# A two-layer decoder trunk: gains and shifts of the residual on GpSimd reordered around the next weight splits, and part of a normalisation moved to ScalarE

## The chip, the cores and the metric

The kernel runs on one core of a Trainium2 chip. The metric is device time in microseconds (us) of one execution, lower is better. The kernel before takes 2448.8 us, the median of three runs (2448.49 to 2449.93). The profile comes from one further execution of 2449.08 us, whose span from the first to the last instruction is 2447.4 us. The engines are named by their short names in the profile: PE is TensorE, PEld its weight load, DVE is VectorE, ACT is ScalarE, POOL is GpSimd, SP is SyncE.

## The reference

Two layers (DEPTH = 2) work on 1024 positions of width 1024. Layer 0 mixes by dilated attention, layer 1 by a spatial gating unit (SGU); both have a cross attention into 256 memory rows, and both end in a SwiGLU feed-forward network (FFN) of width 2816. Every sum is followed by a layer norm.

```python
def layer_norm(x, g, b):
    y = (x - mean(x)) * rsqrt(var(x) + 1e-5)
    return y * g + b

def causal_chunk_sgu(u, v, ln_g, ln_b, w_s, b_s):      # layer 1, width 768
    v = layer_norm(v, ln_g, ln_b)
    mixed = einsum('gts,bnsgc->bntgc', tril(w_s), v in chunks of 128, 12 groups of 64) + b_s
    return u * mixed

for i in range(2):
    ...                                                # mix = attention or SGU of x @ w_in
    y = concatenate([mix, memory_attention]) @ w_out[i]
    x = layer_norm(DN_ALPHA * x + y, ln_mix_g[i], ln_mix_b[i])
    f = (silu(x @ w_gate[i]) * (x @ w_up[i])) @ w_down[i]
    x = layer_norm(DN_ALPHA * x + f, ln_ffn_g[i], ln_ffn_b[i])
```

DN_ALPHA is the square root of 2. What the change touches is the end of the first layer norm of each layer (times g, plus b, then times DN_ALPHA and plus f), and the layer norm of v in the SGU.

## The kernel before, in words

**Numbers.** Every fp32 product is made of three matmuls in a rounded type: both operands are split into a high and a low part, and high·high, low·high and high·low are added in PSUM (`three`, lines 262 to 266). Weights come from HBM in units of 128 x 1024 into a ring of two raw buffers (`load`), and GpSimd splits each unit into `Wh` and `Wl` by two instructions (`split`, lines 253 and 256). A load waits until the unit two before it has been split. Activations are split by ScalarE (high) and VectorE (low).

**Residual.** `XR` holds x as 8 tiles of 128 x 1024. After the output projection it is normalised in place (`out_norm_dve`, `out_norm_act`): ScalarE writes (x - mean) * rstd (line 1018). TensorE then transposes it (line 902), ScalarE and VectorE apply gain and shift by column on the transposed side and split it into `XTh` and `XTl` (`row_act`, `row_dve`). The row-wise gain and shift of `XR` itself, which only the residual sum needs, are done by GpSimd (`norm_pool`, lines 1056 and 1060, with the rows in `gb`) once all 16 pieces of `XTl` are written.

**FFN.** It runs in 11 chunks of 256 hidden columns. A chunk c takes six weight units: gate and up for two column blocks (j = 0 to 3) and two units of w_down (j = 4, 5). TensorE makes four pairs of gate and up (i = 0 to 3, `ffn_pe`), ScalarE the silu (1166) and the high part (1172), VectorE the product `hid` (1179) and the low part (1186). Then TensorE makes 16 products with w_down, and VectorE adds each to `XR` (`acc_dve`): in chunk 0 with the old `XR` times ALPHA (line 870), later by a plain addition (872). Before a pair i, TensorE waits for the `gated` of pair i - 2. The w_gate and w_up slots of a chunk are free for the next chunk's split once the `up` product of its second half is done (`used`).

**SGU.** `wide_pe` makes 24 products of 256 columns for v and then 24 for u. ScalarE applies gelu to v into the 8 tiles of `V` (1265). VectorE takes statistics and, for tiles 0 to 3 and then 4 to 7, writes (v - mean) * rstd (1332) and the gain (1335); the shift is added by GpSimd for tiles 0 to 3 (1392) and by VectorE for 4 to 7 (1338). Then 12 groups are mixed, between the u products 4 to 8 (`MIX_AT`): per group ScalarE writes `VSh` (1292), VectorE `VSl` (1356, it raises `v_low`), TensorE three matmuls, VectorE adds the bias (`gate`, 1344); u products are taken by gelu into one of two buffers `ub` (1281) and multiplied by VectorE (`gated`, 1351). GpSimd splits the last two units of the u weights only when `v_low` has reached 6.

**Order.** Each engine's program is written out by hand and runs in its order; semaphores join them. Nothing is scheduled by a tool.

Of the kernel before, what the change touches and what calls it, by code (L numbers as in the profile page):

```python
# [20 lines left out]
ALU = mybir.AluOpType  # L21
# [52 lines left out]
def build(nc, a, out):  # L74
# [970 lines left out]
    def norm_pool(pool, g, tiles, done=0, last=False):  # L1045
# [3 lines left out]
        for n, t in enumerate(tiles, done):  # L1049
# [9 lines left out]
            pool.wait_ge(*g("gained", n + 1))  # L1059
            nc.gpsimd.tensor_tensor(XR[:, t, :], XR[:, t, :], shift, ALU.add).then_inc(g("shifted"), 1)  # L1060

    def load_cols(eng, g, gain, shift):
        with nc.allow_non_contiguous_dma(reason="1024 gains and shifts, once"):
            for i, w in enumerate((gain, shift)):
                eng.dma_start(gcol[:, i, :], w.rearrange("(k p) -> p k", p=P)).then_inc(g("col_landed"), 16)
# [10 lines left out]
    class Names:  # L1076
# [5 lines left out]
        def __call__(self, name, value=None):  # L1082
# [3 lines left out]

    NORM = {"row_turned": 2 * KT, "affine": 2 * KT, "odd_high": KT, "even_high": KT, "xt_low": 2 * KT, "stats": NT, "root": NT, "partial": 2 * NT, "inverse": NT,
            "rstd": NT, "normed": NT, "gained": NT, "shifted": NT, "gb_landed": 32,
            "col_landed": 32}
    OUT = {**NORM, "product": 16 * KT // 2, "added": 16 * KT // 2}  # L1090
    FFN = {**NORM, "product": 16 * NCH, "added": 16 * NCH,
           **{x: 4 * NCH for x in ("gate", "up", "silu", "gated", "hid_high", "hid_low")}}
# [164 lines left out]
    def sgu_act(act):  # L1257
        act.wait_ge(*at_("mixed", 40))
        act.dma_start(wsraw[:, :, :], a["sgu_w_s"][0].rearrange("g t s -> t g s")).then_inc(gsg("ws_landed"), 16)
        with nc.allow_non_contiguous_dma(reason="1536 biases, once"):  # L1260
            act.dma_start(bst[:, :], a["sgu_b_s"][0].rearrange("g t -> t g")).then_inc(gsg("bs_landed"), 16)

        for n in range(3 * NT):
            act.wait_ge(*gvp("product", n + 1))
            nc.scalar.activation(channels(n), bank(n % 4, M), ACT.Gelu_apprx_tanh).then_inc(gvp("gelu"), 1)
            if n == 9:
                act.wait_ge(*gsg("ws_turned", 1))
                nc.scalar.activation(WSh[:, :, :], ps[:, 2048:2048 + NG * P].rearrange("p (g t) -> p g t", t=P),
                                     ACT.Copy).then_inc(gsg("ws_high"), 1)
                load_gb(act, gsg, a["sgu_ln_g"][0], a["sgu_ln_b"][0], sgb)  # L1270
            if n >= 2 * NT and n % 4 == 3:
                t0 = n % NT - 3
                act.wait_ge(*gsg("stats", t0 + 4))
                nc.scalar.activation(rstd[:, t0:t0 + 4], mv[:, t0:t0 + 4, 1], ACT.Sqrt,
                                     bias=eps[:, 0:1]).then_inc(gsg("root"), 1)

        def gelu(n):
            act.wait_ge(*gup("product", n + 1))
            if n >= 2:
                act.wait_ge(*gup("gated", n - 1))  # L1280
            nc.scalar.activation(ub[:, n % 2, :], bank(n % 4, M), ACT.Gelu_apprx_tanh).then_inc(gup("gelu"), 1)

        gelu(0)
        gelu(1)
        for n in sorted(MIX_AT):
            for i in MIX_AT[n]:
                if i == 0:
                    act.wait_ge(*gsg("shifted", NT // 2))
                    act.wait_ge(*gsg("shifted_late", NT // 2))
                if i >= 2:  # L1290
                    act.wait_ge(*gsg("spatial", i - 1))
                nc.scalar.activation(VSh[:, i % 2, :, :], V[:, :, i * HD:(i + 1) * HD], ACT.Copy
                                     ).then_inc(gsg("v_high"), 1)
            if n == 5:
                gelu(2)
            if n >= 5:
                gelu(n - 2)
        act.wait_ge(*gsg("spatial", NG))
        load_gb(act, go[1], a["ln_mix_g"][1], a["ln_mix_b"][1], gb)

        def turn(t):
            ts = slice(t * P, (t + 1) * P)
            turn_act(act, gup, t, DIL_W // P, 4)
            nc.scalar.activation(XTh[:, 6:8, ts], MO[:, :, ts], ACT.Copy).then_inc(gup("mo_high"), 1)

        for n in range(7, 3 * NT):
            gelu(n)
            if n >= 2 * NT + 2:
                turn(n - 2 * NT - 2)
        turn(NT - 2)  # L1310
        turn(NT - 1)

    def sgu_dve(dve):
        for n in range(3 * NT):
# [7 lines left out]
            if j == 2:  # L1322
                dve.wait_ge(*gsg("partial", n + 1))
                nc.vector.bn_aggr(mv[:, t, :], st[:, t, :, :].rearrange("p a b -> p (a b)")).then_inc(gsg("stats"), 1)
                if t % 4 == 3:
                    t0 = t - 3
                    dve.wait_ge(*gsg("root", t // 4 + 1))
                    nc.vector.reciprocal(rstd[:, t0:t0 + 4], rstd[:, t0:t0 + 4]).then_inc(gsg("rstd"), 1)
                    dve.wait_ge(*gsg("rstd", t // 4 + 1))
                    dve.wait_ge(*gsg("gb_landed", 32))  # L1330
                    for q in range(t0, t0 + 4):
                        nc.vector.tensor_scalar(V[:, q, :], V[:, q, :], mv[:, q, 0:1], rstd[:, q:q + 1], ALU.subtract,
                                                ALU.mult).then_inc(gsg("normed"), 1)
                        dve.wait_ge(*gsg("normed", q + 1))
                        nc.vector.tensor_tensor(V[:, q, :], V[:, q, :], sgb[:, 0, :], ALU.mult).then_inc(gsg("gained"), 1)
                        if q >= NT // 2:
                            dve.wait_ge(*gsg("gained", q + 1))
                            nc.vector.tensor_tensor(V[:, q, :], V[:, q, :], sgb[:, 1, :],
                                                    ALU.add).then_inc(gsg("shifted_late"), 1)
# [123 lines left out]
    def _(pool):  # L1463
# [23 lines left out]
            split(pool, u, attention_over if U_OUT[0] + 3 <= u < U_OUT[0] + 6 else None)  # L1487

        def ffn_units(L):
            for j in range(4):  # L1490
                split(pool, U_FFN[L] + j)
            for j in range(4, 6):
                split(pool, U_FFN[L] + j)
            pool.wait_ge(*go[L]("xt_low", 2 * KT))
            norm_pool(pool, go[L], range(NT))
            with pool.Fori(1, NCH) as c:
                for j in range(6):
                    split(pool, U_FFN[L] + c * 6 + j, used(U_FFN[L] + j, c - 1), (U_FFN[L] + j) % RS,
                          U_FFN[L] // 2 + c * 3 + j // 2 + 1, slot_of(U_FFN[L] + j))
# [15 lines left out]
        for u in range(U_U, U_U + 4):  # L1515
            split(pool, u)
        sgu_pool(pool)
        pool.wait_ge(*gsg("v_low", 6))
        for u in range(U_U + 4, U_FFN[1]):
            split(pool, u)  # L1520
        ffn_units(1)
# [77 lines left out]
    def _(act):  # L1599
# [11 lines left out]
        for L in range(2):  # L1611
# [11 lines left out]
                sgu_act(act)  # L1623
            load_cols(act, go[L], a["ln_mix_g"][L], a["ln_mix_b"][L])
            out_norm_act(act, go[L])
            ffn_first(lambda j: row_act(act, go[L], j), lambda i: ffn_silu(act, L, 0, i), lambda i: ffn_high(act, L, 0, i))
            load_cols(act, gf[L], a["ln_ffn_g"][L], a["ln_ffn_b"][L]) if L == 0 else None
            act.wait_ge(*go[L]("shifted", NT))
# [43 lines left out]
    def _(dve):  # L1672
# [17 lines left out]
        for L in range(2):  # L1690
# [23 lines left out]
                      lambda i: ffn_low(dve, L, 0, i))  # L1714
            for t in range(NT):

                dve.wait_ge(*go[L]("shifted", t + 1))
                acc_dve(dve, gf[L], 0, t, ALPHA)
            with dve.Fori(1, NCH - 1) as c:
                for i in range(4):  # L1720
                    ffn_gated(dve, L, c, i)
# [59 lines left out]
```

## Time and profile before

| quantity | value |
|---|---|
| median of three runs | 2448.8 us |
| the profiled execution | 2449.08 us |
| its span | 2447.4 us |
| PE busy | 2333.3 us, 95% |
| DVE busy | 998.1 us, 41% |
| ACT busy | 599.7 us, 25% |
| POOL busy | 1012.2 us, 41% |
| mean granted PE clock | 0.983 |

PE is busy nearly all the time, so the other engines matter only where PE stands still for them. A granted clock of 1.00 is full speed, 0.50 half speed.

### The profile page before, as it was taken

Reading aid. Unit: us, or ns where it says so; the run is one execution under the profiler, and the core shown is the slowest. Engines: PE = TensorE matmul, PEld = TensorE weight load, DVE = VectorE, ACT = ScalarE, POOL = GpSimd, SP = SyncE. Lnnn points to the kernel's source line nnn. Section 1 sums busy time; section 2 is a strip of 40 time slices with the busy share of each in tenths; the row PEclk is TensorE's granted clock in tenths of the full one; section 3 lists DMA queues with packets and bytes.
Section 4 is the critical chain, followed back from the end, with each engine's and each line's share of the span. In section 5 each row is a group of like instructions: output and inputs, shape, how many; then the busy total and the mean of one; then the engine's idle time right before and its main releaser. Section 6 shows DMA issues by size and latency. Waiting matters only on the chain.

```text
span 2447.4 us, 29983 instructions
## 1 busy us (share of the span) xinstructions
PE 2333.3 (95%) x11608; PEld 1967.2 (80%) x11608; DVE 998.1 (41%) x1931; ACT 599.7 (25%) x1173; POOL 1012.2 (41%) x462
## 2 busy tenths in 40 slices
PE   7999999899999999999998789889999999999997
PEld 6888888678788888888887689878788888888885
DVE  4555555547322222222227536557422222222226
ACT  4656555504100000000005632213200000000003
POOL 3322112653943444333333663434854433333444
PEclk9999999999999999999999989999999999999998
DMA  4111111131111111111111030211021111111111
GB/s 139 61 46 42 44 44 37 59 112 44 44 60 51 51 51 43 43 49 44 44 52 61 9 95 19 70 35 52 27 77 50 44 44 43 43 51 51 51 35 69
DMA packets 160470, 127.63 MB, mean 52 GB/s; under 512 B 11520, under 2 KB 146304, under 8 KB 160384
## 3 DMA queue, kind: packets, MB, share of 16 engines
q1 hardware_dynamic: 147808, 114.31, 15.1%
q10 hardware_dynamic: 12576, 12.16, 1.5%
q8 instruction: 56, 0.92, 0.2%
q14 instruction: 30, 0.25, 0.0%
HBM read 122.26 MB, written 4.19 MB: 52 GB/s over the span
## 4 chain that ended last, share of the span: by engine, by line
PE 83%; DVE 7%; POOL 4%; issue 3%; ACT 3%; DMA 0%; ACTq 0%; DVEq 0%; POOLq 0%
PE ps L264 25%; PE ps L266 25%; PE ps L265 25%; PE ps L552 2%; POOL XR L1056 2%; POOL XR L1060 2%; PE ps L578 1%; PE ps L579 1%; DVE XTl L941 1%; PE ps L539 1%; PE ps L540 1%; DVE XR L872 1%; DVE st L959 1%; PE ps L830 1%; DVE XTh L938 1%
## 5 line engine op out<-in xcount | busy, mean ns | idle before, releaser
L253 POOL TENSOR_TENSOR Wh<-raw,zcol 128x1024 fp32r<-128x1024 f32 x190 | 363.4, 1913 | 1269.7 <-PE ps L266 1234.1
L264 PE MATMUL ps<-XTh,Wh 128*128 128x512 f32 x1760 | 701.6, 399 | 11.9 <-POOL Wl L256 7.3
L266 PE MATMUL ps<-XTh,Wl 128*128 128x512 f32 x1760 | 689.9, 392 | 0.0
L265 PE MATMUL ps<-XTl,Wh 128*128 128x512 f32 x1760 | 689.9, 392 | 0.0
L256 POOL TENSOR_TENSOR Wl<-raw,Wh 128x1024 fp32r<-128x1024 f32 x190 | 470.4, 2476 | 14.9
L264 PEld LDWEIGHTS ps<-XTh,Wh 128*128 128x128 f32 x1760 | 333.0, 189 | 74.8 <-issue 8.2
L266 PEld LDWEIGHTS ps<-XTh,Wl 128*128 128x128 f32 x1760 | 332.4, 189 | 71.0
L265 PEld LDWEIGHTS ps<-XTl,Wh 128*128 128x128 f32 x1760 | 333.3, 189 | 60.2
L872 DVE TENSOR_TENSOR XR<-XR,ps 128x512 f32<-128x512 f32 x416 | 280.9, 684 | 229.0 <-PE ps L266 228.9
L1179 DVE TENSOR_TENSOR hid<-silu,ps 128x512 f32<-128x512 f32 x88 | 60.5, 687 | 737.8 <-PE ps L266 734.1
L264 PE MATMUL ps<-Wh,hidh 128*128 128x512 f32 x704 | 275.6, 391 | 5.1 <-DVE hidl L1186 2.8
L266 PE MATMUL ps<-Wh,hidl 128*128 128x512 f32 x704 | 275.6, 392 | 0.0
L265 PE MATMUL ps<-Wl,hidh 128*128 128x512 f32 x704 | 275.4, 391 | 0.0
L1166 ACT ACTIVATE silu<-ps 128x512 f32<-128x512 f32 x88 | 52.6, 598 | 777.6 <-PE ps L266 777.6
L264 PE MATMUL ps<-Wh,XTh 128*128 128x256 f32 (+1 forms) x640 | 212.0, 331 | 4.8 <-DVE XTl L843 3.6
L265 PE MATMUL ps<-Wl,XTh 128*128 128x256 f32 (+1 forms) x640 | 210.7, 329 | 0.0
L266 PE MATMUL ps<-Wh,XTl 128*128 128x256 f32 (+1 forms) x640 | 210.5, 329 | 0.0
L1172 ACT ACTIVATE hidh<-hid 128x512 fp32r<-128x512 f32 x88 | 55.6, 632 | 458.0 <-DVE hid L1179 458.0
L264 PEld LDWEIGHTS ps<-Wh,hidh 128*128 128x128 f32 x704 | 133.1, 189 | 33.5 <-issue 5.9
L265 PEld LDWEIGHTS ps<-Wl,hidh 128*128 128x128 f32 x704 | 133.0, 189 | 27.7
L266 PEld LDWEIGHTS ps<-Wh,hidl 128*128 128x128 f32 x704 | 132.8, 189 | 27.7
L264 PEld LDWEIGHTS ps<-Wh,XTh 128*128 128x128 f32 x640 | 123.2, 192 | 16.0 <-DVE XTl L843 3.8
(152 smaller groups left out, 2579.2 us busy)
## 6 DMA issues: line engine op xcount, KB each, us to landing
raw<-in_w_gate SPq DMA_DIRECT2D x44, 512.0 KB, 3.8
raw<-in_w_up SPq DMA_DIRECT2D x44, 512.0 KB, 3.8
raw<-in_w_down SPq DMA_DIRECT2D x44, 512.0 KB, 3.4
raw<-in_a_w_in SPq DMA_DIRECT2D x20, 512.0 KB, 3.8
raw<-in_w_out SPq DMA_DIRECT2D x16, 512.0 KB, 3.4
raw<-in_b_w_in SPq DMA_DIRECT2D x14, 512.0 KB, 3.8
B<-in_c_bias SPq DMA_DIRECT2D x12, 512.0 KB, 3.4
raw<-in_w_mem_kv SPq DMA_DIRECT2D x8, 512.0 KB, 4.6
```

Source lines behind the costliest of these rows:

```text
L253: nc.gpsimd.tensor_tensor(Wh[:, slot, :], raw[:, turn, :], zcol[:, 0:1].to_broadcast([P, UNIT]), ALU.add).then_inc(high_done, 1)
L256: nc.gpsimd.tensor_tensor(Wl[:, slot, :], raw[:, turn, :], Wh[:, slot, :].bitcast(F32), ALU.subtract).then_inc(split_done, 1)
L264: nc.tensor.matmul(dst, wh, xh, start=first, stop=False)
L265: nc.tensor.matmul(dst, wh, xl, start=False, stop=False)
L266: return nc.tensor.matmul(dst, wl, xh, start=False, stop=last)
L552: mm = nc.tensor.transpose(bank(4 + gi % 2, P, x * P), probs_of(g, 2 * s + ab, (lo + k) * P, (lo + k + 1) * P), ident[:, :])
L872: nc.vector.tensor_tensor(x, x, bank(4 + n % 4), ALU.add).then_inc(g("added"), 1)
L1056: nc.gpsimd.tensor_tensor(XR[:, t, :], XR[:, t, :], gain, ALU.mult).then_inc(g("gained"), 1)
L1060: nc.gpsimd.tensor_tensor(XR[:, t, :], XR[:, t, :], shift, ALU.add).then_inc(g("shifted"), 1)
L1166: nc.scalar.activation(silu[:, i % 2, :], bank(2 * (i % 2)), ACT.Silu).then_inc(g("silu"), 1)
L1172: nc.scalar.activation(hidh[:, m, h * 512:(h + 1) * 512], hid[:, i % 2, :], ACT.Copy).then_inc(g("hid_high"), 1)
L1179: nc.vector.tensor_tensor(hid[:, i % 2, :], silu[:, i % 2, :], bank(2 * (i % 2) + 1), ALU.mult).then_inc(g("gated"), 1)
```

## The change

The FFN part, in both layers. GpSimd's order was: splits of chunk 0; gain and shift of tiles 0 to 7 alternately; splits of chunk 1. It is now: splits of chunk 0; eight gains; the splits of the gate and up units of chunk 1; eight shifts; the two w_down splits of chunk 1. Since the sum x = ALPHA * XR + f of chunk 0 now comes before the shift, the shift is added behind it, and its row is multiplied by ALPHA by one new ScalarE instruction. VectorE's first additions wait for the gain alone; both VectorE and ScalarE wait for all eight shifts before their loop over chunks 1 to 9.

The SGU part, in layer 1. For tiles 4 to 7 ScalarE does (v - mean) * rstd in place of VectorE, with a new VectorE instruction that makes -mean * rstd for the four tiles; ScalarE does it ahead of its first two gelus of u. GpSimd splits the last two u units when `v_low` has reached 12, not 6.

```diff
+    def gains_pool(pool, g):
+
+        pool.wait_ge(*g("gb_landed", 32))
+        for t in range(NT):
+            nc.gpsimd.tensor_tensor(XR[:, t, :], XR[:, t, :], gb[:, 0, :], ALU.mult).then_inc(g("gained"), 1)
+
+    def shifts_pool(pool, L):
+
+        pool.wait_ge(*go[L]("gb_scaled", 1))
+        for t in range(NT):
+            pool.wait_ge(*gf[L]("added", 2 * t + 2 + gf[L].credit))
+            nc.gpsimd.tensor_tensor(XR[:, t, :], XR[:, t, :], gb[:, 1, :], ALU.add).then_inc(go[L]("shifted"), 1)
...
+        act.wait_ge(*gsg("nmr", 1))
+        act.wait_ge(*gsg("normed", 4))
+        for q in range(4, NT):
+            nc.scalar.activation(V[:, q, :], V[:, q, :], ACT.Identity, bias=nmr[:, q:q + 1],
+                                 scale=rstd[:, q:q + 1]).then_inc(gsg("normed"), 1)
         gelu(0)
         gelu(1)
...
+                    if t0:
+                        nc.vector.scalar_tensor_tensor(nmr[:, t0:t0 + 4], mv[:, t0:t0 + 4, 0], -1.0, rstd[:, t0:t0 + 4],
+                                                       ALU.mult, ALU.mult).then_inc(gsg("nmr"), 1)
                     for q in range(t0, t0 + 4):
-                        nc.vector.tensor_scalar(V[:, q, :], V[:, q, :], mv[:, q, 0:1], rstd[:, q:q + 1], ALU.subtract,
-                                                ALU.mult).then_inc(gsg("normed"), 1)
+                        if t0 == 0:
+                            nc.vector.tensor_scalar(V[:, q, :], V[:, q, :], mv[:, q, 0:1], rstd[:, q:q + 1],
+                                                    ALU.subtract, ALU.mult).then_inc(gsg("normed"), 1)
...
         def ffn_units(L):
-            for j in range(4):
-                split(pool, U_FFN[L] + j)
-            for j in range(4, 6):
+            for j in range(6):
                 split(pool, U_FFN[L] + j)
             pool.wait_ge(*go[L]("xt_low", 2 * KT))
-            norm_pool(pool, go[L], range(NT))
-            with pool.Fori(1, NCH) as c:
+            gains_pool(pool, go[L])
+            for j in range(4):
+                split(pool, U_FFN[L] + 6 + j, U_FFN[L] + j)
+            shifts_pool(pool, L)
+            for j in range(4, 6):
+                split(pool, U_FFN[L] + 6 + j, U_FFN[L] + j)
+            with pool.Fori(2, NCH) as c:
...
         sgu_pool(pool)
-        pool.wait_ge(*gsg("v_low", 6))
+        pool.wait_ge(*gsg("v_low", NG))
...
             out_norm_act(act, go[L])
+            act.wait_ge(*go[L]("gb_landed", 32))
+            nc.scalar.activation(gb[:, 1, :], gb[:, 1, :], ACT.Copy, scale=ALPHA).then_inc(go[L]("gb_scaled"), 1)
...
             for t in range(NT):
 
-                dve.wait_ge(*go[L]("shifted", t + 1))
+                dve.wait_ge(*go[L]("gained", t + 1))
                 acc_dve(dve, gf[L], 0, t, ALPHA)
+            dve.wait_ge(*go[L]("shifted", NT))
```

The order of GpSimd's instructions where the FFN of a layer begins, in the kernel before. The first row is the low part of the last split of chunk 0, L1056 is a gain, L1060 a shift, and L1496 the start of the loop that splits chunk 1 and later.

```order
L256 TENSOR_TENSOR Wl<-raw,Wh 128x1024 [waits high_done]
L1056 TENSOR_TENSOR XR<-XR,gb 128x1024 [waits out_row_turned,out_gb_landed,out_xt_low]
L1060 TENSOR_TENSOR XR<-XR,gb 128x1024 [waits out_gained]
L1056 TENSOR_TENSOR XR<-XR,gb 128x1024 [waits out_row_turned]
...
L1496 UNCONDITIONAL_BRANCH
L1496 ISA
L251 ISA [waits raw_landed0]
L253 TENSOR_TENSOR Wh<-raw,zcol 128x1024 [waits ffn_up]
```

The same place on GpSimd in the changed kernel, where L1066 is a gain, L1073 a shift and L1521 the start of the loop, which now begins with chunk 2.

```order
L1066 TENSOR_TENSOR XR<-XR,gb 128x1024 [waits out_gb_landed,out_xt_low]
L1066 TENSOR_TENSOR XR<-XR,gb 128x1024 x7
L253 TENSOR_TENSOR Wh<-raw,zcol 128x1024 [waits ffn_up,raw_landed0]
L256 TENSOR_TENSOR Wl<-raw,Wh 128x1024 [waits high_done]
...
L1073 TENSOR_TENSOR XR<-XR,gb 128x1024 [waits ffn_added,out_gb_scaled]
L1073 TENSOR_TENSOR XR<-XR,gb 128x1024 [waits ffn_added] x7
L253 TENSOR_TENSOR Wh<-raw,zcol 128x1024 [waits ffn_product,raw_landed0]
...
L1521 UNCONDITIONAL_BRANCH
```

Four splits of chunk 1 have moved ahead of the eight shifts, and two stand behind them; each shift has gained a wait for VectorE's additions.

ScalarE's instructions in the SGU of the changed kernel, from the square root for tiles 4 to 7 on: L1299 is the new normalisation, L1294 the gelu of u with its table, L1310 the first `VSh`. In the kernel before, the table load followed the square root at once.

```order
L1287 ACT_TABLE_LOAD
L1287 ACTIVATE rstd<-mv,eps 128x4 [waits sgu_stats]
L1299 ACTIVATE V<-V,nmr,rstd 128x768 [waits sgu_normed,sgu_nmr]
L1299 ACTIVATE V<-V,nmr,rstd 128x768 x3
L1294 ACT_TABLE_LOAD
L1294 ACTIVATE ub<-ps 128x256 [waits uproj_product] x2
L1310 ACTIVATE VSh<-V 128x512 [waits sgu_shifted_late,sgu_shifted]
```

VectorE's instructions at the same place: L1357 is the gain of one of the tiles 4 to 7, L1360 its shift, and the new L1350 stands where the first of four normalisations stood.

```order
L1346 RECIPROCAL rstd<-rstd 128x4 [waits sgu_root]
L1350 SCALAR_TENSOR_TENSOR nmr<-mv,rstd 128x4 [waits sgu_gb_landed,sgu_rstd]
L1357 TENSOR_TENSOR V<-V,sgb 128x768 [waits sgu_normed]
L1360 TENSOR_TENSOR V<-V,sgb 128x768 [waits sgu_gained]
L1357 TENSOR_TENSOR V<-V,sgb 128x768 [waits sgu_normed]
```

Each tile now costs VectorE two instructions where it had three, and the two gelus of u stand behind four new ScalarE instructions.

## Rows read from the trace of the kernel before

**Rows 1.** Waits of PE: line and releaser, us in total, times, longest.

```profile
PE ps L264 <- POOL Wl L256: 7.3, 2, 3.7
PE ps L264 <- DVE VSl L1356: 6.9, 5, 2.3
```

**Rows 2.** Timeline of PE, layer 0, chunk 0 to 1: start, duration, [idle before].

```profile
659.37 0.39 PE L266 MATMUL ps<-Wh,hidl 128*128 128x512 f32 x1
663.41 0.79 PE L264 MATMUL ps<-XTh,Wh 128*128 128x512 f32 x1 [3.66 <-POOL Wl L256]
667.03 0.40 PE L264 MATMUL ps<-XTh,Wh 128*128 128x512 f32 x1
```

**Rows 3.** Windows there: length, busy us of PE, PEld, DVE, ACT, POOL, PEclk, DMA.

```profile
660.00:667.00 7.00, 3.59 (x9) 2.86 (x10) 0.48 (x1) 0.00 (x0) 6.84 (x4) 0.76 0.52 150
696.00:740.00 44.00, 44.00 (x195) 36.45 (x195) 14.29 (x20) 2.46 (x4) 26.28 (x12) 1.00 0.20 60
```

**Rows 4.** Timeline of POOL, layer 0: first gain, first two splits of chunk 1.

```profile
614.20 2.36 POOL L1056 TENSOR_TENSOR XR<-XR,gb 128x1024 f32<-128x1024 f32 x1 [17.76 <-DVE XTl L941]
...
654.64 1.89 POOL L253 TENSOR_TENSOR Wh<-raw,zcol 128x1024 fp32r<-128x1024 f32 x1
...
658.97 1.89 POOL L253 TENSOR_TENSOR Wh<-raw,zcol 128x1024 fp32r<-128x1024 f32 x1
```

**Rows 5.** Timeline of DVE, layer 0: last addition of chunk 0, hid of chunk 1.

```profile
659.79 0.69 DVE L870 SCALAR_TENSOR_TENSOR XR<-XR,ps 128x512 f32<-128x512 f32 x1 [0.60 <-PE ps L266]
676.14 0.69 DVE L1179 TENSOR_TENSOR hid<-silu,ps 128x512 f32<-128x512 f32 x1 [15.66 <-PE ps L266]
...
687.02 0.69 DVE L1179 TENSOR_TENSOR hid<-silu,ps 128x512 f32<-128x512 f32 x1 [8.34 <-PE ps L266]
```

**Rows 6.** Timeline of ACT, layer 0: last two normalisations, two groups of row pieces.

```profile
600.74 2.38 ACT L1018 ACTIVATE XR<-XR,nmr,rstd 128x1024 f32<-128x1024 f32 x2
603.94 1.45 ACT L927 ACTIVATE fbuf<-ps,gcol 128x512 f32<-128x512 f32 x2 [0.83 <-PE ps L902]
...
609.11 1.45 ACT L927 ACTIVATE fbuf<-ps,gcol 128x512 f32<-128x512 f32 x2 [1.05 <-PE ps L902]
```

**Rows 7.** Timeline of PE in the SGU: mixes of groups 0, 3 and 11.

```profile
1519.76 0.66 PE L264 MATMUL ps<-VSh,WSh 128*128 128x512 f32 x1 [2.31 <-DVE VSl L1356]
...
1524.00 0.50 PE L264 MATMUL ps<-VSh,WSh 128*128 128x512 f32 x1
...
1548.86 0.50 PE L264 MATMUL ps<-VSh,WSh 128*128 128x512 f32 x1 [1.79 <-DVE VSl L1356]
```

**Rows 8.** Timeline of DVE in the SGU: normalisation, last shift, VSl, gated.

```profile
1507.70 0.68 DVE L1332 TENSOR_SCALAR V<-V,mv,rstd 128x768 f32<-128x768 f32 x1
...
1517.14 0.96 DVE L1338 TENSOR_TENSOR V<-V,sgb 128x768 f32<-128x768 f32 x1
1518.93 1.29 DVE L1356 TENSOR_TENSOR VSl<-V,VSh 128x512 fp32r<-128x512 f32 x2 [0.83 <-ACT VSh L1292]
...
1530.57 3.88 DVE L1356 TENSOR_TENSOR VSl<-V,VSh 128x512 fp32r<-128x512 f32 x2
1534.37 2.61 DVE L1351 TENSOR_TENSOR V<-V,ub 128x256 f32<-128x256 f32 x1
...
1548.73 0.41 DVE L1351 TENSOR_TENSOR V<-V,ub 128x256 f32<-128x256 f32 x1
```

**Rows 9.** Timeline of POOL in the SGU: first and last instruction of four splits.

```profile
1527.03 2.01 POOL L253 TENSOR_TENSOR Wh<-raw,zcol 128x1024 fp32r<-128x1024 f32 x1 [20.25 <-DVE VSl L1356]
...
1545.57 2.69 POOL L256 TENSOR_TENSOR Wl<-raw,Wh 128x1024 fp32r<-128x1024 f32 x1
```

**Rows 10.** Timeline of ACT in the SGU: last gelu of v, table, first VSh.

```profile
1503.10 0.38 ACT L1265 ACTIVATE V<-ps 128x256 f32<-128x256 f32 x1 [2.50 <-PE ps L266]
...
1507.47 1.28 ACT L1281 ACT_TABLE_LOAD   x1
...
1518.19 1.15 ACT L1292 ACTIVATE VSh<-V 128x512 fp32r<-128x512 f32 x2 [8.77 <-DVE V L1338]
```

More of the change, by code:

```diff
@@ L1088, in build @@
             "rstd": NT, "normed": NT, "gained": NT, "shifted": NT, "gb_landed": 32,
-            "col_landed": 32}
+            "col_landed": 32, "gb_scaled": 1}
     OUT = {**NORM, "product": 16 * KT // 2, "added": 16 * KT // 2}
@@ L1330, in sgu_dve @@
                     dve.wait_ge(*gsg("gb_landed", 32))
+                    if t0:
+                        nc.vector.scalar_tensor_tensor(nmr[:, t0:t0 + 4], mv[:, t0:t0 + 4, 0], -1.0, rstd[:, t0:t0 + 4],
+                                                       ALU.mult, ALU.mult).then_inc(gsg("nmr"), 1)
                     for q in range(t0, t0 + 4):
-                        nc.vector.tensor_scalar(V[:, q, :], V[:, q, :], mv[:, q, 0:1], rstd[:, q:q + 1], ALU.subtract,
-                                                ALU.mult).then_inc(gsg("normed"), 1)
+                        if t0 == 0:
+                            nc.vector.tensor_scalar(V[:, q, :], V[:, q, :], mv[:, q, 0:1], rstd[:, q:q + 1],
+                                                    ALU.subtract, ALU.mult).then_inc(gsg("normed"), 1)
                         dve.wait_ge(*gsg("normed", q + 1))
                         nc.vector.tensor_tensor(V[:, q, :], V[:, q, :], sgb[:, 0, :], ALU.mult).then_inc(gsg("gained"), 1)
-                        if q >= NT // 2:
+                        if t0:
                             dve.wait_ge(*gsg("gained", q + 1))
```

## The prediction, made before the changed kernel had run

> **What bounds the kernel now.** I read the page first, for the busy shares: PE is busy 95% of the span, so time can only be won where PE stands still or runs slowly. Next I read PE's waits by releaser. Two of the groups are touched by the change: PE waits twice for GpSimd's weight split, 7.3 us, and five times for the low part VSl in the SGU, 6.9 us [rows 1]. Then I went to these places in the timelines. The rest of PE's waits (attention, the turns between stages) is at lines that the change leaves alone.
>
> The first place is the step from chunk 0 to chunk 1 of each FFN. The last matmul of chunk 0 starts at 659.37, the first of chunk 1 at 663.41, after 3.66 us of idle time released by GpSimd's Wl [rows 2]. After the stop PE also runs slowly: the granted clock is 0.76 over the 7 us that hold the stop, and 1.00 later on [rows 3]. Matmuls of 512 columns follow each other at 0.227 us when PE is warm (44 us of the window 696 to 740 hold 195 records of nearly all such matmuls [rows 3]).
>
> The second place is the mixing of the 12 groups in the SGU. PE waits 2.31 us before group 0 and is held up again until group 11 [rows 7]. VectorE is the engine waited for, and its instructions there are long: two VSl take 1.29 us at 1518.93 but 3.88 us at 1530.57, and one gated takes 0.41 us at 1548.73 but 2.61 us at 1534.37 [rows 8]. What differs is GpSimd, which is idle at 1518.93 and at 1548.73 and splits four units from 1527.03 to 1548.26 [rows 9].
>
> **The change part by part.**
>
> *FFN, the stop of PE.* Before, eight gains and eight shifts occupy GpSimd from 614.20 to 654.64, so 2.53 us each, and a split takes 4.33 us (658.97 - 654.64) [rows 4]. PE needs two splits, ready at 663.3. Now only the eight gains stand ahead: 614.2 + 8 x 2.53 = 634.4. The first two splits end at 634.4 + 2 x 4.33 = 643.1, the third and fourth at 651.8. The slots are free in time: the first two splits need the third pair of chunk 0, the other two the fourth, and all pairs are over before the 16 products, which take 16 x 6 x 0.227 = 21.8 us up to 659.6, so by 637.8. The raw data of the first two units landed long ago; for the third and fourth the same ring at the same pace of 4.33 us applies as after 654.64, where GpSimd shows no wait [rows 4]. PE wants the first two at 659.6, so it has 16 us to spare and goes on without a stop. What is won per layer: 663.41 - 659.37 - 0.23 = 3.81 us of stop, and in the slow stretch 667.03 - 663.41 = 3.62 us for nine matmuls that take 9 x 0.227 = 2.04, so 1.58 us [rows 2]. Together 5.39 us, twice 10.8 us. The step from chunk 1 to 2, at the loop's end, runs with PE busy throughout [rows 3], so I give the loop's start no hidden cost.
>
> *FFN, what is late next.* The eight shifts follow at 651.8. The last needs the addition that ended at 660.5 [rows 5] and is reached at 651.8 + 7 x 2.53 = 669.5, so it waits for nothing; all end at 672.0. Behind that wait stand, on ScalarE, one DMA issue and the silu of chunk 1's pair 0, and on VectorE its hid. The gate product will be ready at 665 and the silu is late by 7 us: hid at about 672.0 + 0.6 + 0.1 = 672.7, over at 673.4. PE asks for it only before pair 2, two pairs after 659.6. A pair takes 10.88 us (687.02 - 676.14 [rows 5]), so at 681.4: 8 us to spare. The two w_down splits end at 672.0 + 8.7 = 680.7, and PE asks for them after four pairs, at 703. Cost 0; with the cover gone each us beyond these margins would be a us of stop. VectorE's own additions are not delayed: the gain of tile t is done by 634.4, and the first of the 16 products is over at 637.8 + 1.36 = 639.2.
>
> *FFN, the new ScalarE instruction.* It has the size of line 1018, 1.19 us each [rows 6]. It starts at 603.12, where ScalarE is idle for 0.83 us, and ends at 604.3, so the first row pieces start 0.37 us late. Before the second group ScalarE waits 1.05 us for PE [rows 6]; the 0.37 goes into that. Cost 0; between 0 and 0.4 us a layer.
>
> *SGU, the normalisation.* Before, VectorE works on tiles 4 to 7 from 1507.70 to 1518.10 [rows 8], and ScalarE starts VSh at 1518.19, after 8.77 us of idle [rows 10]. Now VectorE makes one small instruction (0.2 us, my estimate for four elements a row), to 1507.9. ScalarE's first tile takes 3/4 of 1.19 plus its fixed part, 0.93 us, so the first gain starts at 1508.95. Then VectorE has two instructions of 0.96 us a tile, 8 x 0.96 = 7.7 (0.97 x 8 with the gaps). It ends at 1516.65 and not 1518.10: 1.45 us won. The four ScalarE instructions end at 1511.65, the table load takes 1.28 us [rows 10], and gelu 0 is over at 1513.3. PE needs it before u product 4, which starts four products of 2.88 us after 1502.9 (2.88 is ScalarE's rhythm, 2.50 idle and 0.38 busy [rows 10]), at 1514.4. It is in time by 1.1 us. Cost 0; if these instructions ran at 1.24 us each, still 0.
>
> *SGU, the first four groups.* Mix 0 moves from 1519.76 to 1518.3. PE's idle time before it shrinks from 2.31 to 0.9 us. Mixes 0 to 3 took 4.24 us from start to start (1519.76 to 1524.00 [rows 7]), slower than the 3 x 0.69 they need: partly PE's slow clock after the stop, partly the chain VSh, VSl, mix with two buffers. With the chain at warm speed I count 3.7 us. Won here: 1.45 + 0.55 = 2.0 us. Unknown is whether the clock holds: bounds 1.4 and 2.3.
>
> *SGU, groups 4 to 11.* Now GpSimd waits for the twelfth VSl, so it is idle in this whole stretch. Before, from the end of mix 3 (1524.8) to the end of mix 11 (1549.66, 0.8 after its start in rows 7) are 24.86 us. PE's own work there is four products and eight mixes: 4 x 2.88 + 8 x 0.69 = 17.0. Per product and pair of mixes VectorE has two VSl (1.3), one gated (0.41) and two gates (1.4), 3.1 us against PE's 4.26. So at undisturbed lengths VectorE keeps up, and 7.8 us go. Bounds: nothing from a part of it if the order of the hand-overs matters, so 6 to 7.9.
>
> *SGU, the splits behind it.* PE starts product 5 at 1524.8 - 2.0 = 1522.8; three products and six mixes later, at 1535.6, mix 9 is over, and a gate and two VSl (0.7 and 1.3) bring the twelfth VSl to 1537.6. The four splits took 21.2 us before with collisions (1527.03 to 1548.26 [rows 9]); they now run in 17.4 to 21 us, from 1537.7 to 1556. The first two end at 1546.4; PE needs them for u product 16, eight products after product 8 (which ends at 1538.4, before the last mixes), at 1559.9. In time by 13 us. But these splits now stand beside gated 5 to 10. One of these takes up to 2.61 us [rows 8], less than the 2.88 of a product, and two buffers lie between. I follow the first: gate 11 ends at 1540.7, gated 5 comes through when GpSimd's instruction ends, at 1542.7, gelu 7 at 1543.1, and PE wanted it at 1542.7. Cost 0.4 us, bounds 0 and 2.
>
> By the Trainium skill (SBUF — State Buffer, section SBUF: two separate sides), VectorE with two SBUF inputs and a GpSimd instruction exclude each other: whichever starts first keeps the shared ports for its whole length. The trace agrees: 2.61 us is one GpSimd instruction waited for plus 0.41 of its own. The same page speaks against the change in that it moves the collision rather than removes it; by it alone every gated beside a split would take up to 2.7 us, which is the rival below.
>
> **Sum.** 10.8 + 2.0 + 7.8 - 0.4 = 20.2 us less. From the profiled execution of 2449.08 us that gives 2428.9 us; this execution lies 0.3 us above the median of the runs, so I say 2428.8.
>
> **The rivals.**
>
> *The collision is moved.* Gated and VSl slow down because of GpSimd's splits, and the four splits are still there. If VectorE falls behind in gated 5 to 10 as it did in the mixes, PE loses in this stretch what it lost before, up to 6.3 us. For it: lengths of 2.61 and 3.88 us in rows 8. Against it: there is only one such instruction per 2.88 us of PE's work now, not three. Time: 2428.8 + 6 = 2435.
>
> *Only one of the two parts pays.* The FFN part may be given back if PE meets another wait in chunk 1, such as for pair 2; or the SGU part, if gelu 0 or the table is late. If the FFN part brings half, 2428.8 + 5.4 = 2434; if it brings nothing, 2439.6. Against it are margins of 8 and 16 us.
>
> *The change doesn't do what it says.* The stop at chunk 1 remains, because the splits of chunk 1 wait for raw data or for slots until the shifts are through. The stop would stay 3.66 us, the SGU's 9.4 us would be won: 2439.4. Rows 4 speak against it.
>
> *Slower: the shift gate.* All of chunk 1's silu and hid now stand behind the eighth shift. The hand-over from it to PE's pair 2 takes 1.4 us, so PE stops once the shifts end after 680.0. To eat the 5.4 us of its layer they would have to end at 685.4, and to make the whole kernel slower they must also eat the half of the SGU's gain, 4.7 us, so end after 690.1, 18 us later than the 672.0 worked out. Twenty-four instructions of 1.9 to 2.5 us lie between 614.2 and there, and each would have to take 0.75 us more. The longest collisions in the stretch before are already in its mean of 2.53. If they did end at 693, the time would be 2454.
>
> **How the numbers follow.** The forecast has 0.78, its own range 2426 to 2433: the bounds are 2.3 and 1.4 for the first groups, 7.9 and 6 for the others, 0 and 2 for the moved collision, and 0 to 0.8 for the scaling. The moved collision has 0.09, only one part paying 0.06, the stop that remains 0.03, the shift gate 0.02, and 0.02 is left for causes that I don't see. Differences within 0.2% (4.9 us) of 2448.8 are what a measurement of this kernel can't tell from none. All but the last two cases lie beyond this on the fast side. Faster 0.96, same 0.02, slower 0.02. The range that holds 8 in 10, with the nearer part of the moved collision: 2425 to 2435.
>
> **What would show it.** PE's waits after the change: no line for Wl at the step to chunk 1, and the windows there at clock 1.00. GpSimd: gains from 614.2 to 634.4, four splits to 651.8, shifts to 672.0. VectorE's hid of chunk 1's pair 0 at about 673 and PE without a wait before pair 2. In the SGU: first VSh at 1516.7 less the 5.4 us of layer 0, VSl at 0.65 us each throughout, mix 11 ending near 1539.8 - 5.4, and one or two gated of 2.6 us behind it. It would be wrong if PE shows new waits for gated, gelu or hid, if the four ScalarE tiles take over 1.3 us each, or if the clock falls before mix 0.

## The result and the profile after

The changed kernel takes 2425.11 us, the median of four runs (2424.09 to 2426.58). The kernel before took 2449.36 us in the runs that go with them (2448.49 to 2451.92), so the change takes off 24.2 us. The ratio is 0.990, with a 95% interval of 0.9883 to 0.9917. I had forecast 2428.8 us, which is 20.0 us off the 2448.8 of the table. The direction and both mechanisms held. The gain was 4 us larger than forecast: the measured time lies 0.1 us inside the lower end of my range of 2425, and taken as a ratio of 2448.8 (2424.3) it lies outside. One run of the kernel `fn` below, 3356.55 us at a granted clock of 0.652, is left out of its median.

The page of the changed kernel, busy time by engine, and its chain of waits by engine:

```profile
PE 2323.6 (96%) x11608; PEld 1960.2 (81%) x11608; DVE 996.9 (41%) x1928; ACT 606.3 (25%) x1179; POOL 1010.5 (42%) x462
...
PE 88%; DVE 6%; ACT 3%; issue 3%; POOL 0%; DMA 0%; ACTq 0%; DVEq 0%
```

In the chain POOL has gone from 4% to 0% and PE from 83% to 88%. PE's own busy time fell by 9.7 us with the same number of matmuls. That is no saved work: some of these matmuls ran at full clock where they had run at half.

To see where the time went I cut both spans at the same nine instructions, each from the timelines. Times are us.

| from ... to | before | after | difference | forecast |
|---|---|---|---|---|
| start to the first silu of layer 0 (614.55; 614.31) | 614.55 | 614.31 | -0.24 | 0 |
| to the silu of pair 1, chunk 1 (681.53; 675.89) | 66.98 | 61.58 | -5.40 | -5.39 |
| to the high part of the memory rows (1338.07; 1330.84) | 656.54 | 654.95 | -1.59 | 0 |
| to the root for tiles 4 to 7 (1507.16; 1500.08) | 169.09 | 169.24 | +0.15 | 0 |
| to the first VSh (1518.19; 1509.51) | 11.03 | 9.43 | -1.60 | -1.45 |
| to the first turn's XTl in the SGU (1580.42; 1563.33) | 62.23 | 53.82 | -8.41 | -7.95 |
| to the first silu of layer 1 (1724.35; 1707.18) | 143.93 | 143.85 | -0.08 | 0 |
| to the silu of pair 1, chunk 1 (1792.69; 1768.73) | 68.34 | 61.55 | -6.79 | -5.39 |
| to the end (2447.4; 2423.4) | 654.71 | 654.67 | -0.04 | 0 |

The sum is 24.0 us against 20.2. Most of the difference is in two lines, the third and the eighth.

**FFN.** GpSimd in layer 0 of the changed kernel, answering to [rows 4]: start, duration, [idle before].

```profile
613.96 20.21 POOL L1066 TENSOR_TENSOR XR<-XR,gb 128x1024 f32<-128x1024 f32 x8 [17.78 <-DVE XTl L941]
634.13 1.89 POOL L253 TENSOR_TENSOR Wh<-raw,zcol 128x1024 fp32r<-128x1024 f32 x1
...
643.51 1.90 POOL L253 TENSOR_TENSOR Wh<-raw,zcol 128x1024 fp32r<-128x1024 f32 x1 [0.35 <-DMA raw<-in_w_gate]
...
652.17 18.90 POOL L1073 TENSOR_TENSOR XR<-XR,gb 128x1024 f32<-128x1024 f32 x8
671.00 1.92 POOL L253 TENSOR_TENSOR Wh<-raw,zcol 128x1024 fp32r<-128x1024 f32 x1
```

The gains end at 634.1 (I had 634.4), the four splits at 652.2 (651.8), the shifts at 671.0 (672.0). The third split waits 0.35 us for its raw data, which I had put at nothing; PE does not wait for it. PE at the step from chunk 0 to chunk 1, answering to [rows 2], and the granted clock behind it, answering to [rows 3]:

```profile
659.15 0.39 PE L266 MATMUL ps<-Wh,hidl 128*128 128x512 f32 x1
659.38 0.39 PE L264 MATMUL ps<-XTh,Wh 128*128 128x512 f32 x1
```

```profile
663.00:665.00 2.00, 2.00 (x10) 1.68 (x9) 0.00 (x0) 0.00 (x0) 2.00 (x2) 1.00 0.00 0
665.00:667.00 2.00, 2.00 (x10) 1.65 (x10) 0.00 (x0) 0.00 (x0) 2.00 (x2) 1.00 0.00 0
```

The matmuls follow each other at 0.23 us across the step, at clock 1.00. What is late next, as forecast, is the silu and hid of chunk 1's pair 0, held by the eighth shift. ScalarE's scaled shift row and this silu, then VectorE's hid:

```profile
602.75 1.04 ACT L1652 ACTIVATE gb<-gb 128x1024 f32<-128x1024 f32 x1
603.70 1.44 ACT L927 ACTIVATE fbuf<-ps,gcol 128x512 f32<-128x512 f32 x2
...
671.72 0.60 ACT L1179 ACTIVATE silu<-ps 128x512 f32<-128x512 f32 x1 [32.49 <-POOL XR L1073]
```

```profile
672.35 0.69 DVE L1192 TENSOR_TENSOR hid<-silu,ps 128x512 f32<-128x512 f32 x1 [12.09 <-ACT silu L1179]
```

PE asks for this hid two pairs of 10.88 us after 659.4, at 681.1, so it had 8.1 us to spare and did not wait.

**SGU.** PE's waits among the twelve mixes, answering to [rows 7]. These three are all that is left:

```profile
1511.08 0.47 PE L264 MATMUL ps<-VSh,WSh 128*128 128x512 f32 x1 [0.71 <-DVE VSl L1378]
1513.47 0.50 PE L264 MATMUL ps<-VSh,WSh 128*128 128x512 f32 x1 [0.77 <-DVE VSl L1378]
1514.72 0.50 PE L264 MATMUL ps<-VSh,WSh 128*128 128x512 f32 x1 [0.28 <-DVE VSl L1378]
```

VectorE, answering to [rows 8], and ScalarE, answering to [rows 10]:

```profile
1501.88 0.96 DVE L1357 TENSOR_TENSOR V<-V,sgb 128x768 f32<-128x768 f32 x1 [1.09 <-ACT V L1299]
...
1516.39 1.28 DVE L1378 TENSOR_TENSOR VSl<-V,VSh 128x512 fp32r<-128x512 f32 x2
1517.59 0.75 DVE L1373 TENSOR_TENSOR V<-V,ub 128x256 f32<-128x256 f32 x2
...
1533.43 6.79 DVE L1373 TENSOR_TENSOR V<-V,ub 128x256 f32<-128x256 f32 x4
```

```profile
1500.82 3.79 ACT L1299 ACTIVATE V<-V,nmr,rstd 128x768 f32<-128x768 f32 x4 [0.44 <-DVE nmr L1350]
1504.62 1.28 ACT L1294 ACT_TABLE_LOAD   x1
1505.92 0.66 ACT L1294 ACTIVATE ub<-ps 128x256 f32<-128x256 f32 x2
1509.51 1.15 ACT L1310 ACTIVATE VSh<-V 128x512 fp32r<-128x512 f32 x2 [2.93 <-DVE V L1360]
```

Two VSl take 1.28 us and two gated 0.75 us, where one gated had taken 2.61. The collision has moved, as one of the rivals said: behind the mixes four gated take 6.79 us. But PE has no wait there: between 1500 and 1582 its waits are the three above, 1.8 us in all.

### The profile page after: what moved, and what is told of

It reads as the page before. It is cut to its first block, busy times and chain, and to the rows that moved or that the text cites. A ratio compares the mean times of both kernels' runs of the same rounds, so it can differ in the third digit from the quotient of the medians.

```text
span 2423.4 us, 29967 instructions
## 1 busy us (share of the span) xinstructions
PE 2323.6 (96%) x11608; PEld 1960.2 (81%) x11608; DVE 996.9 (41%) x1928; ACT 606.3 (25%) x1179; POOL 1010.5 (42%) x462
## 4 chain that ended last, share of the span: by engine, by line
PE 88%; DVE 6%; ACT 3%; issue 3%; POOL 0%; DMA 0%; ACTq 0%; DVEq 0%
PE ps L264 27%; PE ps L266 26%; PE ps L265 26%; PE ps L552 2%; PE ps L578 1%; PE ps L579 1%; PE ps L539 1%; PE ps L540 1%; DVE XTl L941 1%; DVE XR L872 1%; DVE st L959 1%; PE ps L830 1%; DVE V L1357 0%; DVE XTh L938 0%; ACT PTh L670 0%
```

## The experiments

**Each part alone.** The first four kernels take the parts of the change apart.

`f_only`: the FFN part alone.

```diff
-        act.wait_ge(*gsg("nmr", 1))
-        ...                                   # ScalarE's normalisation of tiles 4 to 7 back on VectorE
-        pool.wait_ge(*gsg("v_low", NG))
+        pool.wait_ge(*gsg("v_low", 6))
```

> Only the FFN part of the change (gains, four splits, shifts, in both layers); the SGU as before. Theory A (stop and slow matmuls as the trace of before shows them in each layer, 5.4 in layer 0 and 6.8 in layer 1, 14 slow matmuls there and not 8): 12.2 us less than before, 13.8 if PE's clock no longer falls at the end of layer 0; 2435.6 to 2437.2. Theory B (the forecast's 5.39 twice): 10.8 us less, 2438.6. Rival (the shift gate bites): under 8 us less.

Measured: 2436.09 us, ratio 0.9944 (0.9932 to 0.9957), which is 12.9 us less than the 2448.95 of its runs. Between the same marks as in the table, layer 0's step is 5.44 us shorter and layer 1's 6.80 us. This is theory A; the shift gate does not bite. The stretch up to the memory rows is 1.50 us shorter, though nothing was changed in it, and the one from the memory rows to the root is 2.26 us longer than before. The edit touches neither. The second stretch comes in two sizes over all twelve profiles of this text, 169.1 to 169.3 us in six and 170.8 to 171.4 us in the other six, so a profile alone can be 2 us off there.

`w_only`: GpSimd's wait alone.

```diff
-        pool.wait_ge(*gsg("v_low", 6))
+        pool.wait_ge(*gsg("v_low", NG))
```

> Only GpSimd's wait for the twelfth v_low in place of the sixth; the rest as before. Theory: the collisions of VSl and gated with the weight splits are the whole loss from mix 4 to mix 11, so 7.8 us less than before (2441.6), VSl at 0.65 us each there, and the gated products behind it up to 2.6 us long with no wait of PE. Rival (the collision is moved): at most 2 to 3 us less.

Measured: 2440.57 us, ratio 0.9964 (0.9951 to 0.9977), 8.4 us less. From the first VSh to the first turn it takes 54.47 us, 7.76 less than before; forecast was 7.8. PE's waits for VSl fall to the two ahead of mix 3, with the stop before mix 0 still 2.3 us long:

```profile
PE ps L264 <- DVE VSl L1356: 2.5, 2, 2.3
```

A further 1.39 us came off at layer 1's step from chunk 0 to 1 and 1.6 us at the end of layer 1, where this kernel is the kernel before.

`n_only`: the normalisation alone.

```diff
+        for q in range(4, NT):
+            nc.scalar.activation(V[:, q, :], V[:, q, :], ACT.Identity, bias=nmr[:, q:q + 1],
+                                 scale=rstd[:, q:q + 1]).then_inc(gsg("normed"), 1)
         gelu(0)
...                                            # and VectorE's part as in the change
```

> Only the normalisation of value tiles 4 to 7 on ScalarE; the rest as before. Theory: first VSh 1.6 us earlier, PE's wait before mix 0 falls from 2.3 to 0.7 us, its clock stays up, mix 0 to 3 0.6 us shorter: 2.2 us less, 2447.2. Rival: the collisions behind it with GpSimd's splits, which now start earlier by as much, take it back or add to it: 2449.4 plus or minus 1.

Measured: 2445.4 us, ratio 0.9986 (0.9978 to 0.9995), 3.5 us less with an interval from 1.2 to 5.4. The first VSh comes 1.60 us earlier relative to the root, as expected. But from VSh to the first turn it takes 0.90 us more than before, not 0.6 less. The mixes themselves are 0.6 us shorter; the loss lies behind them, where PE's clock fell after the last of the collision's stops. PE at mix 11 and after, and the window:

```profile
1546.58 0.50 PE L264 MATMUL ps<-VSh,WSh 128*128 128x512 f32 x1 [1.78 <-DVE VSl L1365]
...
1547.62 0.42 PE L264 MATMUL ps<-Wh,XTh 128*128 128x256 f32 x1
1547.83 0.42 PE L265 MATMUL ps<-Wl,XTh 128*128 128x256 f32 x1
```

```profile
1545.00:1550.00 5.00, 3.42 (x15) 3.20 (x16) 4.49 (x8) 1.10 (x3) 0.98 (x1) 0.71 0.52 158
```

Matmuls of 256 columns come at 0.21 us there, against 0.12 at full clock. So alone this edit nets 0.7 us in the trace. The trace is 3.5 us shorter than that of before, like the runs, and the rest lies where the edit touches nothing: 1.4 us at layer 1's step from chunk 0 to 1, with 7 slow matmuls behind the stop and not 14, and 1.6 us at the end of layer 1. The measured time fits neither number that I had written down, and the 3.5 us are not the value of this edit.

`fn`: the changed kernel without the wait.

```diff
-        pool.wait_ge(*gsg("v_low", NG))
+        pool.wait_ge(*gsg("v_low", 6))
```

> The changed kernel with GpSimd's wait set back to the sixth v_low. Theory: the wait is worth 7.8 us here as well, so 2425.1 + 7.8 = 2432.9. Rival (the wait matters little once VectorE has less to do): 2425 to 2428.

Measured: 2433.86 us, the median of five runs, ratio 0.9938 (0.9925 to 0.9951), 8.8 us above the changed kernel. From the first VSh to the first turn it takes 63.16 us against 53.82: the wait is worth 9.3 us here, 7.8 for the collision and 1.5 for the clock that falls behind mix 11 as in `n_only`. The rival, that the wait no longer matters, is ruled out.

**The clock.** Two profiles differed by 1.6 us where no instruction was changed, at the end of layer 0. There PE stops for 2.1 us in both. PE after this stop before the change, and its clock:

```profile
1304.36 1.55 PE L902 MATMUL ps<-ident,XR 128*128 128x128 f32 x8 [2.10 <-DVE XTh L938]
1305.55 0.78 PE L264 MATMUL ps<-XTh,Wh 128*128 128x512 f32 x1
1306.13 0.63 PE L265 MATMUL ps<-XTl,Wh 128*128 128x512 f32 x1
```

```profile
1306.00:1308.00 2.00, 2.00 (x6) 1.52 (x6) 1.53 (x3) 0.43 (x1) 0.00 (x0) 0.50 0.49 134
```

And the same place in the changed kernel:

```profile
1298.73 1.09 PE L902 MATMUL ps<-ident,XR 128*128 128x128 f32 x8 [2.08 <-DVE XTh L938]
1299.58 0.48 PE L264 MATMUL ps<-XTh,Wh 128*128 128x512 f32 x1
1299.90 0.39 PE L265 MATMUL ps<-XTl,Wh 128*128 128x512 f32 x1
```

```profile
1300.40:1302.40 2.00, 2.00 (x10) 1.66 (x9) 1.53 (x3) 0.43 (x1) 0.00 (x0) 1.00 0.40 118
```

After 2.10 us of idle time the granted clock is 0.50 (1.2 GHz), after 2.08 us it is 1.00 (2.4 GHz). Before the change a slow stretch follows this stop and the next one, of 2.8 us; in the changed kernel only the second has one. To see whether this hangs on the length of the stop or on something else, I shifted the program by a few matmuls.

`ph4` and `ph9`: the changed kernel with extra matmuls in layer 0. `bph9`: the kernel before with the same nine.

```diff
+            if first and L == 0 and i == 1:
+                for _ in range(9):            # 4 in ph4
+                    nc.tensor.matmul(bank(2), wtile(sl[2], 0)[0], XTh[:, 0, 0:512], start=True, stop=True)
             for j, name in enumerate(("gate", "up")):
```

> The changed kernel with 4 extra matmuls on PE ahead of pair 1 of chunk 0 in layer 0 (they are written over), so that all behind them comes 0.91 us later. Theory (whether PE's clock falls after a stop of some 2 to 4 us depends on the moment of the stop, not on its length): the stops keep their lengths, and slow stretches appear or vanish: at the stops of 2.1 and 2.8 us at the end of layer 0 and at those in the SGU's turns; 2426.0 plus 0 to 3. Rival (the clock depends on the length of the stop alone): the same slow stretches as in the changed kernel, 2426.0.

> As the one before, with 9 extra matmuls, so 2.04 us. Theory: slow stretches at other stops than in the changed kernel, 2427.1 plus 0 to 3. Rival: 2427.1 with the same stretches.

> The kernel before with 9 extra matmuls at the same place. Theory: the slow stretches of 5 matmuls after the 2.1 us stop at the end of layer 0 and of 14 after the 3.7 us stop in layer 1 change in length or go: 2.04 more, less up to 3.0. Rival: both stay as they are, exactly 2.04 us more (2451.4).

Measured, one run each: 2427.26, 2430.44 and 2445.91 us. `ph4` is 2.2 us above the changed kernel's median for 0.91 us of added work, `ph9` 5.3 for 2.04, a little beyond the 5.0 that I had allowed. `bph9` is 3.2 us below the 2449.13 of the kernel before although it has 2.04 us more to do, and 2.3 us below the least that I had allowed. These times are not the doing of the added matmuls alone. Up to these matmuls every kernel here runs the same program, and yet, with the added work taken off, the first silu of layer 0 comes between 611.7 us (`bph9`) and 615.8 us (`ph9`); before the change it came at 614.55. So 2.9 of the 5.2 us that `bph9` gained lie ahead of the edit. What follows rests on the stretches and not on the times. The stops at the end of layer 0 are 2.1 and 2.8 us long in `ph4` and `ph9` as well, but against the changed kernel the slow stretch has moved from behind the second to behind the first. `bph9` shows the same. The windows behind the 2.1 us stop of `ph4` and `ph9`:

```profile
1300.00:1303.00 3.00, 3.00 (x9) 2.37 (x8) 2.30 (x4) 0.97 (x2) 0.25 (x1) 0.53 0.46 131
```

```profile
1303.00:1306.00 3.00, 3.00 (x11) 2.35 (x10) 2.41 (x3) 0.56 (x2) 0.66 (x1) 0.55 0.34 99
```

In `bph9` the 3.67 us stop in layer 1 is unchanged, but a slow run of 7 matmuls follows it and not of 14. Before and `bph9`:

```profile
1777.00:1779.00 2.00, 2.00 (x6) 1.52 (x6) 0.00 (x0) 0.00 (x0) 1.29 (x2) 0.50 0.31 51
```

```profile
1777.00:1779.00 2.00, 2.00 (x11) 1.64 (x10) 0.00 (x0) 0.00 (x0) 1.65 (x2) 1.00 0.24 38
```

`again`: the changed kernel once more, not a line different.

> The changed kernel once more, for a second profile. Theory (the moment of a stop against something that runs independently of the program decides on slow stretches): the stops are the same to 0.1 us, the slow stretches differ from those of the first profile, the time 2424 to 2428. Rival (they are fixed by the program): the same stretches, of 7 matmuls behind the 2.8 us stop, none behind the 2.1 us stop, 7 before the output projection of layer 1.

Measured: 2426.98 us, ratio 0.9908 (0.9891 to 0.9924). The stops are the same (2.1, 2.8, 3.3 us), the slow stretches are not: there is none behind either of the first two, where the first profile has one behind the second. The windows behind the 2.8 us stop in the first profile, then those behind the 2.1 and the 2.8 us stop in `again`:

```profile
1312.00:1314.00 2.00, 2.00 (x7) 1.51 (x6) 0.69 (x1) 0.12 (x1) 0.17 (x1) 0.50 0.91 303
```

```profile
1300.00:1303.00 3.00, 3.00 (x16) 2.50 (x15) 2.42 (x3) 0.55 (x2) 0.67 (x1) 1.00 0.32 90
1312.00:1315.00 3.00, 3.00 (x15) 2.47 (x14) 1.94 (x3) 0.60 (x1) 0.67 (x1) 1.00 0.98 275
```

Each such stretch costs 1.6 us: from chunk 1 to the memory rows it is 656.5 us with both (before), 655.0 with one (changed) and 653.3 with none (`again`).

So behind the stop of 2.8 us neither the length of the stop nor the program decides: both are the same in these two profiles. Behind longer stops the clock was regular: over all twelve profiles it fell behind each of the stops of 3.3, 3.6, 3.7 and 6.2 us, and only how many matmuls were slow varied. Nor is it shown that the program has no part at the 2.1 us stop: the three profiles whose layer 0 is that of before (before, `w_only`, `n_only`) all have the stretch behind the 2.1 us stop, and the five whose layer 0 is that of the change with nothing added (changed, `again`, `f_only`, `fn`, `quiet`) all lack it. That it hangs on the moment of the stop against something independent of the program would fit all of this, but it was not measured and stays open.

**The shift gate.** `late` puts the shifts behind all six splits.

```diff
-            for j in range(4):
+            for j in range(6):
                 split(pool, U_FFN[L] + 6 + j, U_FFN[L] + j)
             shifts_pool(pool, L)
-            for j in range(4, 6):
-                split(pool, U_FFN[L] + 6 + j, U_FFN[L] + j)
```

> The changed kernel with all six splits of chunk 1 ahead of the eight shifts. The two w_down splits wait for the 16th product (659.6 in layer 0), end at 668.3, and the shifts at 687.2. Theory (the shift gate of the fourth rival, from the trace of the changed kernel): hid of pair 0 ends at 688.6, TensorE wanted it at 681.1, so it stops 7.5 us in each layer, and its clock falls, 1.6 to 3 us more: 2425.1 + 18 to 21, 2443 to 2446. Rival (the gate does not bind, TensorE has other work): 2425.

Measured: 2446.56 us, ratio 0.9988 (0.9979 to 0.9998), 21 us above the changed kernel and 0.6 us above the upper end of what I had expected. The gate is real. The shifts end at 686.0, and PE stops for hid before pair 2, 7.8 us in layer 0 and 8.2 us in layer 1. GpSimd and PE's waits in layer 0 (the 9.2 us hold 1.4 that every version has):

```profile
667.31 18.71 POOL L1073 TENSOR_TENSOR XR<-XR,gb 128x1024 f32<-128x1024 f32 x8
```

```profile
PE ps L264 <- DVE hid L1192: 9.2, 2, 7.8
```

**Where the collision still costs.** With the mixes freed, PE's longest stops near the SGU are two at its end, 2.7 and 3.6 us, where GpSimd's splits for the output projection meet VectorE's last gated and XTl. `quiet` holds these splits back.

```diff
         for u in range(U_U + 4, U_FFN[1]):
+            if u == U_OUT[1] + 4:
+                pool.wait_ge(*gup("mo_low", NT))
             split(pool, u)
```

> The changed kernel, where GpSimd splits units 4 and 5 of the layer 1 output projection only when VectorE has made the last low part of the SGU's turns; TensorE needs them 43 us later. Theory (the collision with the splits holds up the chain of gated, XTl and turns): PE's two waits there, 2.7 and 3.6 us, shrink by 1.2 and 1.7: 2.9 us less, 2422.2, or 4.4 less if its clock stays up. Rival (the waits are the latency of the chain itself): within 0.5 us of 2425.1.

Measured: 2421.33 us (2420.27 to 2424.56), ratio 0.9886 (0.9869 to 0.9902). This is the fastest of all versions, 3.8 us under the changed kernel's median. The intervals of the two ratios overlap, so by the runs alone it is likely and not certain; in the trace the stretch from the first turn (transpose) to the first silu of layer 1 is 140.96 us against 143.85, 2.89 less, as worked out. PE's waits there, after the change and in `quiet`:

```profile
PE ps L264 <- DVE XTl L843: 3.6, 1, 3.6
PE ps L830 <- DVE XTl L843: 2.7, 1, 2.7
```

```profile
PE ps L264 <- DVE XTl L843: 1.9, 1, 1.9
PE ps L830 <- DVE XTl L843: 1.6, 1, 1.6
```

## What of the prediction held, and which steps failed

The mechanisms held: both waits went as written, and the moved collision and the shift gate did not bind. What failed is the price of PE's slow clock behind a stop. The step that wrote 1.58 us of slow matmuls "twice" had layer 1 wrong, where the trace of before has 2.95 us, and the clock behind stops that stay was put at nothing, where 1.6 us came off at the end of layer 0. Together these are 3.0 of the 3.8 us by which the trace gained more than forecast.

*The stop at chunk 1.* Right in layer 0 to 0.01 us (5.40 against 5.39), with GpSimd's order, the warm clock and the 8 us of slack as written. Wrong in layer 1 by 1.4 us, and this is the first mis-sized term: I worked out the slow matmuls behind the stop in layer 0 (1.58 us) and wrote "twice". In layer 1 the trace of before shows 14 slow matmuls where layer 0 has 7 (the expectation of `f_only` says 8, which is a miscount), from 1773.21 to 1779.33 us, 6.12 us for 3.17 us of work, so 2.95. The rows were there to read. The size varies from execution to execution: `bph9`, `w_only` and `n_only` have about 7 at the same stop. A bound of 1.5 to 3 us per stop was due, and I gave none.

*A term that was missing.* 1.6 us came off at the end of layer 0, behind a stop that I had set aside because the change leaves its line alone. The stop is still there; the clock did not fall behind it. The prediction priced the clock only where it took away a stop. `again`, `ph4` and `ph9` show that stops of 2.1 and 2.8 us carry such a stake, and that runs of one program differ in it. The stretch behind the 2.1 us stop is there in all three profiles with the old layer 0 and missing in all five with the new one, so these 1.6 us may be the change's own by its timing. Why the clock fell in the ones and not in the others stays open.

*The normalisation.* 1.60 us against 1.45. ScalarE took 0.95 us a tile, gelu 0 was over at 1506.3 and PE asked at 1507.3 (the last gelu of v at 1496.02 less 0.2, plus four products of 2.88), 1.0 us of slack where I had 1.1.

*Mixes 0 to 3.* Start to start they took 3.64 us (1511.08 to 1514.72) against 4.24 before and 3.7 forecast; the clock held after the shorter stop, as chosen between the bounds.

*Groups 4 to 11.* Forecast 7.8 us; `w_only` has 7.76. The cause was tested in both directions, by `w_only` and `fn`. The second gave 9.3 in the trace and 8.8 in the runs; its trace also has a slow stretch behind mix 11 that before does not have.

*The moved collision.* I charged 0.4 us with bounds 0 and 2; it cost nothing. Gated does run at a quarter of its speed there (6.79 us for four, where four take 1.7 undisturbed), but PE, with two gelu buffers and four banks between, does not wait. The rule cited from the Trainium skill (SBUF — State Buffer, SBUF: two separate sides), that the two engines exclude each other for a whole instruction, agrees with these lengths, on average 1.70 us for 0.42 us of work. The upper end that the prediction drew from it, 2.7 us, is too low by its own working: 2.69 us of waiting and 0.41 of work make 3.1. The price is set by who waits for the instruction. `quiet` is the same collision with someone waiting: 2.89 us.

*The rivals.* "Only one of the two parts pays" fell: 12.9 us and 8.4 us came alone. "The stop remains" fell with PE's row at 659.38. The shift gate did not bind in the changed kernel, and `late` shows its price: the shifts ended at 686.0, 15 us later than in the changed kernel, and the whole gain was gone but for 2 us. The prediction's rule for this price, one us for each us beyond 680.0, was too low. It gives 6.0 us in layer 0 at 686.0, or 7.0 since the profile of `late` runs 1.0 us ahead of that of the changed kernel at the first silu. The stop was 7.8 us, and from the first silu to the memory rows `late` took 10.1 us more than the changed kernel, as slow matmuls follow the stop; layer 1, from its first silu to the end, shows 10.1 us as well. The failed step is the same as above: the clock behind a stop.

*The range.* The bounds of the terms add up to 21.0 us at most, so 2427.8; the 2426 and 2425 that I wrote lie below that with no working. That the measured 2425.11 came out beside 2425 is therefore luck. The clock behind the stops was left out; with 1.5 us a stop at the four stops concerned the lower end would have been near 2422. The 2428.8 itself has a slip: 2428.9 less 0.3 is 2428.6.

## What to carry to other kernels

Ask of each piece of a helper engine's work when its result is first needed, and put first what the bounding engine asks for first; here a sum was reordered (gain, product, then scaled shift) so that half of the work could go behind the weights. Where two engines exclude each other, move the one with slack out of the other's latency chain, and price a collision by who waits for it, not by how much the instruction stretches. When a stop goes, price it as its idle time plus the slow matmuls behind it, read each occurrence of the stop in the trace, and leave 1.5 us either way for each of 2 to 3 us that stays.

## What the runs showed of the hardware

Whether PE's clock falls behind a stop of 2 to 3 us is not repeatable. Over the twelve profiles it fell in six behind the 2.1 us stop at the end of layer 0 and in eight behind the next one, of 2.8 to 2.9 us; in `again`, the same program, it did not fall where it had in the first profile. Behind the stops of 3.3, 3.6, 3.7 and 6.2 us it fell each time. Between 0 and 14 matmuls of 512 columns ran at half speed behind such stops, up to 2.95 us.

The same program differs from run to run early on too: in the five profiles that run the changed kernel's program up to there (changed, `again`, `f_only`, `fn`, `quiet`) the first silu of layer 0 came between 612.3 and 614.8 us. So a difference of 2 to 5 us between two versions of this kernel, in one run each, says nothing without the stretch that it comes from.

VectorE's product of two operands in SBUF takes 0.42 us alone and 2.61 us beside GpSimd's splits (128x256), and the split costs time only where PE waits for that product.
